# Whole 128-column inverse factors in a recurrence's solve, and two groups of products issued for two heads in turn

## What is computed

```python
def rwkv7_recurrence(r, w, k, v, a, b):
    def step(state, inp):
        r_t, w_t, k_t, v_t, a_t, b_t = inp
        sa = jnp.einsum('bhvk,bhk->bhv', state, a_t)
        state = (state * w_t[:, :, None, :] + sa[..., None] * b_t[:, :, None, :]
                 + v_t[..., None] * k_t[:, :, None, :])
        return state, jnp.einsum('bhvk,bhk->bhv', state, r_t)
    ...
# hgrn2_mixer: S_t = diag(f_t) S_{t-1} + (1 - f_t) i_t^T, o_t = S_t^T q_t
```

## Time and profile before

| | us |
|---|---|
| median of 3 runs | 1341.31 |
| lowest and highest | 1339.23, 1341.62 |
| the profiled execution | 1340.01 |
| its span (first to last instruction) | 1338.2 |
| PE busy | 1294.5 (97%) |
| DVE, ACT, POOL busy | 836.8, 692.7, 117.7 |

### The profile page before, as it was taken

The page is one execution under the profiler, slowest core; times in us unless marked ns, Lnnn a source line. Parts: engine busy times, 40 slices in busy tenths (PEclk is TensorE's granted clock), DMA queues, the critical chain, the costliest instruction groups (busy, mean ns, idle before and its releaser), DMA issues.

```text
span 1338.2 us, 24943 instructions
## 1 busy us (share of the span) xinstructions
PE 1294.5 (97%) x10580; PEld 1170.1 (87%) x10580; DVE 836.8 (63%) x1257; ACT 692.7 (52%) x894; POOL 117.7 (9%) x75
## 2 busy tenths in 40 slices
PE   5999999999999999999999999999999999999997
PEld 4998998889999999999888888999999899888886
DVE  3557756886656977646655544646878746755533
ACT  2456535765766566234544434766567334544432
POOL 0000000000001330221100000000430130200000
PEclk9899999999999999989999999999999999999999
DMA  9667754724434433125455554434443214555542
GB/s 387 236 265 264 270 196 160 261 91 159 158 127 158 158 127 126 66 78 169 168 185 189 189 189 130 158 137 146 155 152 126 67 70 158 191 178 184 187 164 88
DMA packets 35103, 222.94 MB, mean 167 GB/s; under 512 B 3888, under 2 KB 8240, under 8 KB 9264
## 3 DMA queue, kind: packets, MB, share of 16 engines
q1 hardware_dynamic: 30384, 215.05, 45.4%
q10 hardware_dynamic: 4608, 6.29, 1.4%
HBM read 220.28 MB, written 1.05 MB: 165 GB/s over the span
## 4 chain that ended last, share of the span: by engine, by line
PE 86%; DVE 7%; ACT 4%; DMA 1%; issue 1%; SPq 0%; POOL 0%; ACTq 0%; DVEq 0%
PE pj L612 56%; PE yv L612 14%; PE sc L612 9%; PE tp L612 5%; DVE ring_rounded L711 3%; ACT w_split L702 1%; PE tp L481 1%; DMA big<-weights 1%; PE tp L1757 1%; DMA ring<-weights 1%; DVE att_area L555 1%; DVE big L1720 1%; DVE rw L1548 0%; ACT att_area L511 0%; DVE yT_rounded L1712 0%
## 5 line engine op out<-in xcount | busy, mean ns | idle before, releaser
L711 DVE TENSOR_TENSOR ring_rounded<-ring,w_split 128x2048 fp32r<-128x2048 f32 x108 | 255.8, 2371 | 60.5 <-ACT w_split L702 58.2
L702 ACT CAST w_split<-ring 128x2048 fp32r<-128x2048 f32 x108 | 205.4, 1902 | 45.1 <-PE pj L612 28.7
L1969 DVE TENSOR_TENSOR ring_rounded<-ring,big_rounded 128x2048 fp32r<-128x2048 f32 x62 | 142.1, 2292 | 102.4 <-ACT big_rounded L1852 102.3
L612 PE MATMUL pj<-h_split,w_split 128*128 128x256 f32 x1264 | 175.6, 292 | 5.1 <-DVE h_split L2307 2.1
L612 PEld LDWEIGHTS pj<-h_split,w_split 128*128 128x128 f32 x1264 | 159.7, 194 | 13.5 <-issue 9.2
L612 PE MATMUL pj<-h_split,ring_rounded 128*128 128x256 f32 x1264 | 165.3, 283 | 1.9 <-DVE ring_rounded L711 1.9
L612 PEld LDWEIGHTS pj<-h_split,ring_rounded 128*128 128x128 f32 x1264 | 157.0, 190 | 3.1 <-DVE ring_rounded L711 2.8
L1852 ACT CAST big_rounded<-ring 128x2048 fp32r<-128x2048 f32 x66 | 125.8, 1907 | 50.8 <-PE pj L612 49.2
L612 PE MATMUL pj<-hT_rounded,w_split 128*128 128x256 f32 x1136 | 148.7, 284 | 0.0
L612 PEld LDWEIGHTS pj<-hT_rounded,w_split 128*128 128x128 f32 x1136 | 142.2, 193 | 0.0
L1230 POOL TENSOR_TENSOR big<-big 128x512 f32<-128x512 f32 x16 | 31.0, 1939 | 740.1 <-DVE big L1163 728.0
(11 more groups left out here) (365 smaller groups left out, 2240.9 us busy)
## 6 DMA issues: line engine op xcount, KB each, us to landing
ring<-weights SPq DMA_DIRECT2D x180, 1024.0 KB, 4.9
big<-weights SPq DMA_DIRECT2D x20, 1024.0 KB, 7.7
first_block<-biases ACTq DMA_DIRECT2D x32, 192.0 KB, 4.9
xT<-x_t SPq DMA_DIRECT2D x1, 1024.0 KB, 9.6
out_t<-scr SPq DMA_DIRECT2D x4, 256.0 KB, 2.9
con<-constants SPq DMA_DIRECT2D x1, 896.0 KB, 6.7
aux<-small SPq DMA_DIRECT2D x1, 832.0 KB, 10.2
level_masks_sb<-levels SPq DMA_DIRECT2D x1, 672.0 KB, 9.4
```

The lines of the kernel that those rows point to most:

```text
L612: return nc.tensor.matmul(out, lhsT, rhs, start=start, stop=stop, skip_group_check=True)
L702: act.post(nc.scalar.copy(w_split[:, w % 2], ring[:, in_ring(idx)]), s["w_high"])
L711: dve.post(nc.vector.tensor_tensor(ring_r[:, at], ring[:, at], w_split[:, w % 2].bitcast(F32), ALU.subtract), s["w_low"])
L1969: e.tell(engine.tensor_tensor(w_low(t, i), w, value(w_high(i)), ALU.subtract), signal)
```

## The change

The factors of a pair now lie side by side, [i][x][64 columns], with the two families' places exchanged: `inv[:, i, 0]` is what was x = 1 and `inv[:, i, 1]` what was x = 0. Then `whole(i)`, 128 adjacent columns, is the whole transposed inverse of a pair, if the lower rows of `inv[:, i, 0]` are zero. POOL writes those zeros after the corner's products have read them, and PE waits for POOL once more before the right-hand sides. `pe_solve` is one 128x128 product a head. The hgrn outputs and the recurrence's outputs are issued term by term for two heads in turn, their number and operands unchanged. VectorE's and POOL's instructions on `inv` only have other addresses.

```diff
@@ pe_hgrn
-            for h in range(NH):
...
-                matmul(o[:, 0:P], v(0), m(0))
-                matmul(o[:, P:SEQ], v(1), m(1), True, False)
-                last = matmul(o[:, P:SEQ], v(0), flat(h_scx)[:, (2 * (h % 2) + c) * P:(2 * (h % 2) + c + 1) * P], False)
+            for c in range(2):
+                for T, cross in ((0, False), (1, False), (1, True)):
+                    for h in (2 * c, 2 * c + 1):
+                        last = pe_hgrn_value(h, T, cross)
             last.then_inc(s["hgrn_out"].sem, 1)
@@ factors
-        inv = flat(scr[:, :, :])[:, 0:1024].rearrange("p (x i t) -> p x i t", x=2, t=HD)
+        inv = flat(scr[:, :, :])[:, 0:1024].rearrange("p (i x t) -> p i x t", x=2, t=HD)
+        whole = lambda i: flat(scr[:, :, :])[:, i * P:(i + 1) * P]
@@ pe_rwkv
-            pe.take(s["level_masked"])
+            pe.take(s["level_masked"], 2)
             pe.take(s["inverse_level"])
...
-                    i, columns = at(T, h), slice(h * HD, (h + 1) * HD)
-                    matmul(yv[T][upper, columns], inv[upper, 1, i], r_t[upper, 0, columns])
-                    last = matmul(yv[T][lower, columns], inv[:, 0, i], r_t[:, 0, columns])
+                    columns = slice(h * HD, (h + 1) * HD)
+                    last = matmul(yv[T][:, columns], whole(at(T, h)), r_t[:, 0, columns])
...
-            for h in range(NH):
-                o = y_of(h)
-                matmul(o[:, 0:P], vn(0, h), rw[:, 3, at(0, h)], h < 2, False)
...
+            for c in range(2):
+                for n, (columns, term) in enumerate(terms):
+                    for h in (2 * c, 2 * c + 1):
+                        matmul(y_of(h)[:, columns], *term(h), c == n == 0, n == 1)
@@ pool_rwkv
-            pool.tell(nc.gpsimd.tensor_copy(inv[BLOCK_ROWS[1], 0], inv[BLOCK_ROWS[1], 1]), s["level_masked"])
+            lower = BLOCK_ROWS[1]
+            pool.tell(nc.gpsimd.tensor_copy(inv[lower, :, 1], inv[lower, :, 0]), s["level_masked"])
+            pool.take(s["xlx_done"], 2 * LEVELS)
+            pool.tell(nc.gpsimd.memset(inv[lower, :, 0], 0.0), s["level_masked"])
             pool.take(s["inverse_level"])
```

More of the change, by code:

```diff
@@ L1092, in pe_hgrn, with pe_hgrn_value @@
             pe.take(s["hgrn_merged"], 2)
-            for h in range(NH):
+            def pe_hgrn_value(h, T, cross):
                 c, r = h // 2, (h % 2) * HD
-                o = yv[0][r:r + HD, c * SEQ:(c + 1) * SEQ]
-                v = lambda T: hi[:, T, h * HD:(h + 1) * HD]
-                m = lambda T: flat(h_sc[h % 2])[:, (2 * T + c) * P:(2 * T + c + 1) * P]
-                matmul(o[:, 0:P], v(0), m(0))
-                matmul(o[:, P:SEQ], v(1), m(1), True, False)
-                last = matmul(o[:, P:SEQ], v(0), flat(h_scx)[:, (2 * (h % 2) + c) * P:(2 * (h % 2) + c + 1) * P], False)
+                o = yv[0][r:r + HD, c * SEQ + T * P:c * SEQ + (T + 1) * P]
+                if cross:
+                    m = flat(h_scx)[:, (2 * (h % 2) + c) * P:(2 * (h % 2) + c + 1) * P]
+                else:
+                    m = flat(h_sc[h % 2])[:, (2 * T + c) * P:(2 * T + c + 1) * P]
+                return matmul(o, hi[:, 0 if cross else T, h * HD:(h + 1) * HD], m, not cross, cross or T == 0)
+            for c in range(2):
+                for T, cross in ((0, False), (1, False), (1, True)):
+                    for h in (2 * c, 2 * c + 1):
+                        last = pe_hgrn_value(h, T, cross)
             last.then_inc(s["hgrn_out"].sem, 1)
@@ L1336, in pe_rwkv @@
                         for rows in BLOCK_ROWS:
-                            last = matmul(sc[T][rows, h * HD:(h + 1) * HD], level_of(l)[rows, i], inv[rows, 0, i])
+                            last = matmul(sc[T][rows, h * HD:(h + 1) * HD], level_of(l)[rows, i], inv[rows, i, 1])
                     last.then_inc(s["lx_done"].sem, 1)
@@ L1343, in pe_rwkv @@
                         for rows in BLOCK_ROWS:
-                            matmul(tp[T][rows, h * HD:(h + 1) * HD], inv[rows, 1, i], inv_w[rows, i])
+                            matmul(tp[T][rows, h * HD:(h + 1) * HD], inv[rows, i, 0], inv_w[rows, i])
                         for rows in BLOCK_ROWS:
-                            last = matmul(yv[T][rows, h * HD:(h + 1) * HD], inv_w[rows, i], inv[rows, 1, i])
+                            last = matmul(yv[T][rows, h * HD:(h + 1) * HD], inv_w[rows, i], inv[rows, i, 0])
                     last.then_inc(s["xlx_done"].sem, 1)
@@ L1353, in pe_rwkv @@
                     i = T * NH + h
-                    last = matmul(sc[T][lower, h * HD:(h + 1) * HD], lower_corner[:, i], inv[upper, 0, i])
+                    last = matmul(sc[T][lower, h * HD:(h + 1) * HD], lower_corner[:, i], inv[upper, i, 1])
                 last.then_inc(s["lx_done"].sem, 1)
@@ L1359, in pe_rwkv @@
                     i = T * NH + h
-                    last = matmul(yv[T][upper, h * HD:(h + 1) * HD], inv_w[lower, i], inv[lower, 1, i])
+                    last = matmul(yv[T][upper, h * HD:(h + 1) * HD], inv_w[lower, i], inv[lower, i, 0])
                 last.then_inc(s["xlx_done"].sem, 1)
             fill(pe, pe_slot, f"rwkv{layer}", 3 + LEVELS)
-            pe.take(s["level_masked"])
+            pe.take(s["level_masked"], 2)
             pe.take(s["inverse_level"])
@@ L1562, in dve_rwkv @@
                         eye = block_eye.unsqueeze(1).to_broadcast([P, NH, HD])
-                        dve.do(nc.vector.tensor_tensor(inv[:, 0, part], eye, of_heads(tp[T]), ALU.subtract))
-                        ins = nc.vector.tensor_tensor(inv[:, 1, part], eye, level_of(0)[:, part], ALU.subtract)
+                        dve.do(nc.vector.tensor_tensor(inv[:, part, 1], eye, of_heads(tp[T]), ALU.subtract))
+                        ins = nc.vector.tensor_tensor(inv[:, part, 0], eye, level_of(0)[:, part], ALU.subtract)
                     elif l < LEVELS - 1:
-                        dve.do(nc.vector.tensor_tensor(inv[:, 0, part], inv[:, 0, part], of_heads(tp[T]), ALU.subtract))
-                        ins = nc.vector.tensor_tensor(inv[:, 1, part], inv[:, 1, part], of_heads(yv[T]), ALU.subtract)
+                        dve.do(nc.vector.tensor_tensor(inv[:, part, 1], inv[:, part, 1], of_heads(tp[T]), ALU.subtract))
+                        ins = nc.vector.tensor_tensor(inv[:, part, 0], inv[:, part, 0], of_heads(yv[T]), ALU.subtract)
                     else:
-                        ins = nc.vector.tensor_scalar(inv[0:HD, 0, part], of_heads(yv[T])[0:HD], -1.0, None, ALU.mult)
+                        ins = nc.vector.tensor_scalar(inv[0:HD, part, 1], of_heads(yv[T])[0:HD], -1.0, None, ALU.mult)
                     if T == 0:
```

8 lines of the change are left out of this document (4 added, 4 removed).

## The result

The changed kernel takes **1331.54 us** (median of 6 runs, 1328.75 to 1333.87). The kernel before took 1338.09 us in 6 runs beside it (1336.23 to 1341.62). The ratio of the runs is 0.9944, with an interval of 0.9919 to 0.9969: faster by about 0.6% (the medians alone give 0.5%). Part of the miss is plain already: the three runs that the forecast was built on had a median of 1341.31, and the six runs of the same kernel, these three among them, have 1338.09.

The account below looks back on a forecast made before the run. TensorE (PE), 86% of the chain, was taken to bound the kernel. Layer 1's 1.8 us (0.27 + 1.2 + 0.33) and layer 0's 3.1 make 4.9 off 1340.0, 1335.1; with 1.3 for the median, 1336.4 us, range 1333.0 to 1340.0.

Parts of the forecast that it names:

- Decay values: hgrn outputs on PE, issued in turn: 1.72 us becomes 1.45, gain 0.27 us in each layer, bounds 0 and 0.4.
- First solve: PE, 4 full-square products replace 8: 2.05 us becomes 0.90, gain 1.2 us a layer with the shape change, bounds 0.9 and 1.3.
- Second solve and outputs: PE before the bonus product: 5.61 us becomes 3.75, but VectorE's bonus factors limit the gain to 0.33 us.
- POOL's memset: Zeros written ahead of the first right-hand sides: 0.61 us, hidden by branch products, cost 0, at most 0.3 us a layer.
- Layer 0 and the clock: Layer 0's solve stage: if the clock falls to 1.2 GHz at the same time again, gain 3.1 us.
- the base: Starting time for the forecast: the profiled execution's 1340.0 us, plus 1.3 for the median of the runs shown.
- Rival 1: The clock falls in neither layer's stage: gain 6.6 us, 1334.7 us; chance 0.20.
- Rival 2: The clock falls in both layers' stages: layer 1 gives up 1.7 us, gain 3.2, 1338.1 us; chance 0.15.
- Rival 3: Solves with whole factors stay as slow as before: gain about 1.2 us, 1340.1 us; chance 0.06.
- Rival 4: No new PE wait at the bonus: 1.5 us more a layer at full clock, 1334.9 us; chance 0.06.
- Rival 5: The new bonus wait brings 1.2 GHz on gate products, 3.4 us a layer: slower, 1343.8 us; chance 0.05.
- Rival 6: PE's queue already overlaps fully and the memset holds PE; half the solves' gain goes: 1339 us; chance 0.06.

Follow-up runs that it names:

- turns alone: Kernel before with decay values and outputs issued in turn for two heads, solve and factors as before: 1339.85 us, ratio 0.9999.
- early factors on the kernel before: Kernel before with VectorE's two bonus factors moved ahead of the last two branch sums: 1337.8 us, ratio 1.0003.
- whole products twice: Changed kernel with each product of the solves made twice, 8 full-square products a solve, same result: 1333.57 us, ratio 0.9962.
- longer wait: Changed kernel with VectorE computing the two bonus factors twice, so PE idles longer ahead of the bonus product: 1337.12 us, ratio 0.9983.
- old solve twice: Kernel before with each product of the two solves made twice, 16 products a solve, same result: 1357.44 us, ratio 1.0123.
- whole factors alone: Changed kernel with decay values and outputs put back to head by head, one full-square product a head kept: 1332.01 us, ratio 0.9950.
- changed kernel with early factors: Changed kernel with VectorE's two bonus factors ahead of the branch sums and weight remainder, two sets: 1328.52 and 1328.91 us.
- halves with early factors: Changed kernel with whole factors used as two 64-column products in turn and bonus factors ahead of the branch sums: 1327.74 us, ratio 0.9909.
- halves with the wait: Changed kernel with each whole factor multiplied as two 64-column products on the array's column halves in turn: 1333.67 us, ratio 0.9967.

## Why the prediction was wrong

**The sum for layer 1 held, though not each of its terms.** Forecast 1.8 us for layer 1 with its decay values, measured 0.26 + 1.48 = 1.74.

- Decay values: forecast 1.45 us for the 12 pairs, measured 1.46 in both layers. Right.
- First solve: forecast 0.90, measured 0.84. Up to the start of the second solve the stage gained 1.35 us (5.00 instead of 6.35), where 1.2 was forecast.
- Second solve and outputs: PE is through with them after 3.77 us (1074.94 to 1078.71); forecast 3.75. The new wait on the bonus factors is there, forecast 1.5 us, measured 1.71. So this part gained 0.13 us (5.48 instead of 5.61) and not 0.33. The 0.2 come from VectorE: the weight remainder took 2.48 us, the row of before had 2.29. The reason is POOL: its seventh branch addition was still running when the remainder started, until 1076.29; before it was over at 1084.12, ahead of the remainder's start at 1085.20. In the two traces all 192 remainders with no POOL addition beside them took 2.28 or 2.29. The prediction's "nobody in this stretch waits for them", said of these additions, is wrong: VectorE does (last section).
- POOL's memset: forecast at most 0.61 and hidden, measured 0.52 and hidden.

**The wrong step is "Layer 0 and the clock", in "If it falls at the same time again".** It held the slow stretch of layer 0 for something that the change leaves alone, and gave it the same odds with and without the change. The runs show the reverse. The stretch began 1.2 us behind the old solve, and the old solve is what the change takes out. With old factors the time at 1.2 GHz is 30 to 37 us a run (before, turns alone, early factors on the kernel before), 50 with the solve twice; with whole factors it is 23, with the solve twice too (22 to 26 with early factors; 27.5 and 30.3 only where a wait is longer). Of the 8 us between the means, 3.1 to 3.5 are work, where the rows of the trace make 3.5 (2 x 0.26 + 2 x 1.48) and the terms of the forecast at full clock 3.6; 4.5 to 4.9 are clock. The prediction had 1.3 us for the clock, by which layer 0's 3.1 exceeds layer 1's 1.8; in the pair of traces it is 3.05, by which layer 0's stage gained more than layer 1's. How much of the 4.5 to 4.9 lies in the stages over all runs isn't known (see "What stays open").

**The second error is the base.** "The median of the runs shown is 1.3 above that execution" took three runs for the kernel's time. 1341.31 was the median of three draws from a spread that reaches from 1334 to 1348; the 66 later runs have medians of 1336.4 to 1338.2. Of the 4.9 us by which the forecast was too high, 3.2 are the base (1341.3 against 1338.1) and 1.7 the gain (4.9 against 6.55). The range had room for the cases of the clock, and none for this.

**The rivals.** Rival 1, the clock falls in neither layer, is what the trace shows; its gain of 6.6 us stands against 6.55 between the medians of these runs, 7.0 between their means and 8.0 between the means when the kernel was run again. That 1334.7 is still 3 us too high is the base. I gave it 0.20, "the work is lighter still" standing against it: lighter in PE's time, but whole products twice and once have the same clock, so PE's time in the solve is not what the clock goes by. Rival 2 (a fall in both layers) happened in no trace of whole factors without a longer wait. Rival 3 falls: a whole factor runs at the right-hand sides' rate. Rival 4 falls, the wait came. Rival 5, the wait costs clock, is not borne out for the wait of 1.7 us; as a mechanism it was seen behind waits of 2.20 and 2.76 us, though not each time (two of two in one trace, one of two in the other) and for 3.4 us at 1.2 GHz, half of the stretch that it had assumed. It lay closer than its 0.05 said; had the change also halved the solve, it would have met it. Rival 6 falls: the outputs pair up, and PE has no wait on POOL. The Trainium skill ("TensorE: Matmul & The Clock Gate", section "A second HAM failure mode: psum-queue depth-cycling") says that short idling between groups of products can make the clock swing. The stretches behind the waits of 2.2 and 2.76 us agree with that; the falls behind the old solve do not fit it as far as the profile shows, since PE was busy for 12.54 of the 12.60 us ahead of one.

**What stays open.** The granted clock is known here by stretches and by the mean of a run. Which property of the old solve counts (64 rows in half of its products, the change between 64 and 128 rows from product to product, 64 columns, or one product at a time) was not taken apart. The solve by halves, which also has tiles of 64 columns but two of them at a time and the full 128 rows, had 23.0 us without a wait; that speaks against the columns alone. Why some executions have a fall and others of the same kernel have none is open too. Not all of the difference in clock can be placed at the solves either. Only the profiled executions show where their time at 1.2 GHz lies:

| traces | in the two solve stages, us | elsewhere, us |
|---|---|---|
| before; early factors on before; turns alone | 6.8; 0; 13.7 | 30.9; 26.0; 38.8 |
| old solve twice | 30.8 | 27.2 |
| changed kernel (2); whole factors alone; whole products twice | 0 in each | 24.1, 18.9; 21.5; 19.1 |
| changed kernel with early factors (2); halves with early factors | 0 in each | 24.2, 22.5; 26.5 |
| halves with the wait; longer wait | 6.8; 3.4 | 30.0; 27.0 |

"Elsewhere" is the first 60 us, stretches near 200 and 830 us, and the last 5 to 8 us, where nothing is changed; yet the kernels with the old solve have more there too, in these few traces. So the stages show that the clock falls at the old solve (in 4 of 8 layers with it, in none of 14 with whole factors and no longer wait), but how many of the 8 to 10 us by which the means at 1.2 GHz differ come from there is not shown, nor why the rest differs.

## What to carry to other kernels

Where a trace shows a stretch at 1.2 GHz, ask what PE did just ahead of it, and whether the change touches that very work; a run of small-tile products issued one at a time can cost more in clock than in its own length (doubled, the old solve cost 10 us in clock and 7.7 in work). Read the mean clock of every run before a base is chosen, and let the range hold the spread of the base when there are three runs. And when PE's part gets shorter, look at once for what is due next on VectorE and put it earlier: here the cheap move behind the change was worth 3 us, as much as the change's own work at full clock.

## What the runs showed of the hardware

**Column halves in turn with 64 streamed columns** run faster than I had read from the pairs with 128: 16 records in 0.51 and 0.62 us, 0.06 to 0.08 a pair, where the outputs' pairs take 0.12. Full-square products take 0.93 and 0.84 us for the same work. With the shape changes counted the halves are 0.45 us a layer ahead, not the 0.64 of the solves alone.

**A vector instruction with two tensors read waits for a POOL addition that is under way.** Layer 0 of the kernel with the longer wait: VectorE's timeline for the first bonus factor alone and for all four, then POOL's for its additions.

```profile
576.62 1.48 DVE L1584 SCALAR_TENSOR_TENSOR big<-raw,vec 128x256 f32<-128x256 f32 x1
...
576.62 3.05 DVE L1584 SCALAR_TENSOR_TENSOR big<-raw,vec 128x256 f32<-128x256 f32 x4
```

```profile
565.16 12.66 POOL L1739 TENSOR_TENSOR big<-big 128x512 f32<-128x512 f32 x8
```

The last POOL addition in layer 1 of the kernel before, and the last two of the changed kernel, where one alone takes 1.27 us:

```profile
1085.31 3.31 POOL L1729 TENSOR_TENSOR big<-big 128x512 f32<-128x512 f32 x1 [1.20 <-DVE big L1720]
...
1075.02 4.54 POOL L1739 TENSOR_TENSOR big<-big 128x512 f32<-128x512 f32 x2
```

With the longer wait POOL's last addition ends at 577.82 and the first factor at 578.10, 0.28 us later; the three behind it take 0.52 each. In layer 1 of the changed kernel it is the same: POOL ends at 1079.56, the two factors at 1080.36, which is 0.28 + 0.52 on. In the kernel before POOL ends at 1088.62 and the two factors at 1089.42, again 0.28 + 0.52. It goes the other way too: POOL's last addition, begun beside the weight remainder, takes 3.31 and 3.19 us instead of 1.27. So what I called VectorE's chain is in part POOL's: the "2.01 us for two factors" were one factor held up and one at full rate. This is also why the longer wait came out at 2.76 us. The Trainium skill ("SBUF — State Buffer", section "SBUF: two separate sides") says that the port pair of the two engines is an exclusive lock, held for the whole instruction; these rows agree. The early factors don't escape it: in layer 0 of the changed kernel they take 1.17 and 1.38 us, each ending 0.28 behind a POOL addition, but there nobody waits for them. Whether the branch additions on POOL could be moved out of the factors' way was not tried.
